# Prompt attention of a two-layer decoder step: one f32 triangle product per step replaced by two fp32r products of a split operand

## The reference, cut to what matters

```python
def stick_breaking_block(q, k, v, bias, q_pos, k_pos):
    z = (jnp.einsum('bqhd,bkhd->bhqk', q, k).astype(jnp.float32) * (SB_HEAD_DIM ** -0.5)
         + bias.astype(jnp.float32)[None, :, None, None])
    mask = k_pos[None, :] < q_pos[:, None]
    log_keep = jnp.where(mask, jax.nn.log_sigmoid(-z), 0.0)
    between = lax.cumsum(log_keep, axis=3, reverse=True) - log_keep
    a = jnp.where(mask, jnp.exp(jax.nn.log_sigmoid(z) + between), 0.0)
    return jnp.einsum('bhqk,bkhd->bqhd', a.astype(v.dtype), v)
```

## Time and profile before

| | |
|---|---|
| median of 3 runs | 2942.45 us (2940.32 to 2943.23) |
| profiled execution | 2944.57 us |
| its span, first to last instruction | 2942.9 us |
| TensorE busy | 2762.6 us, 94% |
| VectorE busy | 1578.4 us, 54% |
| ACT busy | 968.1 us, 33% |
| POOL busy | 678.6 us, 23% |

### The profile page before, as it was taken

One profiled execution on the slowest core, in us unless ns is written; L12 is line 12 of the kernel. 1 busy time (PEld: TensorE's weight loads), 2 busy tenths in 40 slices (PEclk: granted clock), 3 DMA queues, 4 the chain that ended last, 5 costly groups with the idle time before them and its releaser, 6 DMA issues. The chain is left out here.

```text
span 2942.9 us, 45906 instructions
## 1 busy us (share of the span) xinstructions
PE 2762.6 (94%) x17051; PEld 2367.5 (80%) x17051; DVE 1578.4 (54%) x2496; ACT 968.1 (33%) x1747; POOL 678.6 (23%) x624
## 2 busy tenths in 40 slices
PE   7999999988898899999989999999989999999898
PEld 7988888734444699799749999999967769999567
DVE  5367777788656677452334434333448963351534
ACT  5311121245565111332233323333334442231231
POOL 0001222222231222220002225422237612220020
PEclk9999999989999999999999999999999999999999
DMA  7477998787614711321654233323268864314641
GB/s 271 141 250 250 348 347 315 255 258 224 179 40 150 252 51 30 114 84 52 230 194 136 83 107 120 108 95 107 96 206 274 275 220 166 103 63 154 209 157 66
DMA packets 300161, 498.86 MB, mean 170 GB/s; under 512 B 45113, under 2 KB 175802, under 8 KB 299586
## 3 DMA queue, kind: packets, MB, share of 16 engines
q1 hardware_dynamic: 280642, 429.13, 44.1%
q0 software_dynamic: 15120, 51.46, 5.1%
q10 hardware_dynamic: 4176, 15.32, 1.3%
HBM read 383.06 MB, written 117.00 MB: 170 GB/s over the span
## 5 line engine op out<-in xcount | busy, mean ns | idle before, releaser
L889 PE MATMUL ps<-in_hi,w_halves 128*128 128x344 f32 x1536 | 499.6, 325 | 13.3 <-DVE in_lo L800 13.3
L891 PE MATMUL ps<-in_hi,w_halves 128*128 128x344 f32 x1536 | 494.5, 322 | 0.0
L890 PE MATMUL ps<-in_lo,w_halves 128*128 128x344 f32 x1536 | 494.1, 322 | 0.0
L647 POOL TENSOR_TENSOR w_halves<-w_raw,w_halves 128x1024 fp32r<-128x1024 f32 x60 | 145.9, 2435 | 727.3 <-ACT w_halves L720 727.3
L889 PEld LDWEIGHTS ps<-in_hi,w_halves 128*128 128x128 f32 x1536 | 292.5, 190 | 20.7 <-DVE in_lo L800 19.6
L890 PEld LDWEIGHTS ps<-in_lo,w_halves 128*128 128x128 f32 x1536 | 292.0, 190 | 1.1
L891 PEld LDWEIGHTS ps<-in_hi,w_halves 128*128 128x128 f32 x1536 | 292.2, 190 | 0.0
L1937 PE MATMUL ps<-in_hi,wv_hi 128*128 128x344 f32 x696 | 229.3, 329 | 3.9 <-DVE wv_lo L1785 3.9
L1938 PE MATMUL ps<-in_lo,wv_hi 128*128 128x344 f32 x696 | 224.3, 322 | 0.0
L1939 PE MATMUL ps<-in_hi,wv_lo 128*128 128x344 f32 x696 | 224.2, 322 | 0.0
L488 PE MATMUL ps<-in_hi,w_halves 128*128 128x344 f32 x640 | 204.7, 320 | 0.4 <-DVE w_halves L364 0.4
(11 more groups left out here) (428 smaller groups left out, 6100.9 us busy)
## 6 DMA issues: line engine op xcount, KB each, us to landing
k_pages<-in_cache_k SPq DMA_DIRECT2D x256, 256.0 KB, 4.7
v_pages<-in_cache_v POOLq DMA_DIRECT2D x160, 256.0 KB, 5.5
v_pages<-in_cache_v SPq DMA_DIRECT2D x96, 256.0 KB, 3.0
w_raw<-in_w_c SPq DMA_DIRECT2D x48, 512.0 KB, 3.8
in_raw<-og SPq DMA_DIRECT2D x120, 172.0 KB, 3.5
cc<-residual SPq DMA_DIRECT2D x120, 172.0 KB, 1.9
kq_raw<-in_w_mem SPq DMA_DIRECT2D x32, 512.0 KB, 4.0
w_words<-in_mem_k SPq DMA_DIRECT2D x16, 1024.0 KB, 5.9
```

The source lines that it names most:

```text
L647: return eng.tensor_tensor(w_lo[:, m % KT, :], raw[:, m % RAW, :], w_hi[:, m % KT, :].bitcast(f32), ALU.subtract)
L889: pe.matmul(acc(n), w_hi[:, t, a:b], h, start=(kt == 0), stop=False)
L890: pe.matmul(acc(n), w_hi[:, t, a:b], l, start=False, stop=False)
L891: last = pe.matmul(acc(n), w_lo[:, t, a:b], h, start=False, stop=(kt == KT - 1))
```

## The change

The softplus of a step is split in two. ACT copies it into `sp_hi`, which rounds it to fp32r; the pool engine subtracts that from the softplus into `sp_lo`. The triangle's f32 product becomes two fp32r products, of `sp_hi` and of `sp_lo`, with an fp32r copy of the triangle. The sum waits for `sp_lo`. VectorE's softplus waits for the subtraction of step t-3 in place of the sum. In its round t, ACT does the copy of step t+1 between weight(t-1) and logarithm(t+3). The pool engine does the subtraction of a step ahead of that step's additions.

```diff
-                pe.wait_ge(sp_done, t + 1)
-                last = pe.matmul(o, k.c("neg_tri"), sp_[:, t % 3, n0:512], start=False, stop=top(t), skip_group_check=True)
+                pe.wait_ge(sp_lo_done, t + 1)
+                pe.matmul(o, tri_r[:, :], sp_hi[:, t % 3, n0:512], start=False, stop=False, skip_group_check=True)
+                last = pe.matmul(o, tri_r[:, :], sp_lo[:, t % 3, n0:512], start=False, stop=top(t), skip_group_check=True)
...
-            pe.wait_ge(tables_done, 2)
+            pe.wait_ge(tables_done, 3)
...
-                    dve.wait_ge(sum_done, t - 2)
+                    dve.wait_ge(sp_lo_done, t - 2)
...
+            def softplus_high(t):
+                n0 = n0_of(t)
+                act.wait_ge(sp_done, t + 1)
+                if t >= 3:
+                    act.wait_ge(sum_done, t - 2)
+                act.copy(sp_hi[:, t % 3, n0:512], sp_[:, t % 3, n0:512]).then_inc(sp_hi_done, 1)
...
-            for dst, src in ((ident_r, k.c("ident")), (mask_r, k.sb_mask[:, :])):
+            for dst, src in ((ident_r, k.c("ident")), (mask_r, k.sb_mask[:, :]), (tri_r, k.c("neg_tri"))):
                 act.copy(dst[:, :], src).then_inc(tables_done, 1)
...
             for t in range(3):
                 logarithm(t)
+                if t == 1:
+                    softplus_high(0)
...
                     if t >= 1:
                         weight(t - 1)
+                    if t + 1 < NT_:
+                        softplus_high(t + 1)
                     if t + 3 < NT_:
                         logarithm(t + 3)
...
+            def softplus_low(t):
+                n0 = n0_of(t)
+                pool.wait_ge(sp_hi_done, t + 1)
+                if t >= 3:
+                    pool.wait_ge(sum_done, t - 2)
+                pool.tensor_tensor(sp_lo[:, t % 3, n0:512], sp_[:, t % 3, n0:512], sp_hi[:, t % 3, n0:512].bitcast(f32),
+                                   ALU.subtract).then_inc(sp_lo_done, 1)
+
             for t in range(NT_):
+                softplus_low(t)
                 if not last_block(t):
                     later(t)
```

More of the change, by code:

```diff
@@ L1005, in sb_prompt @@
         vtok = sb("vtok", [128, 2, T // 128, 128])
-        ident_r, mask_r = (sb(n, [128, 128], f32r) for n in ("ident_r", "mask_r"))
+        ident_r, mask_r, tri_r = (sb(n, [128, 128], f32r) for n in ("ident_r", "mask_r", "neg_tri_r"))
         zc = sb("zc", [128, 3, 512])
         sp_ = sb("softplus", [128, 3, 512])
+        sp_hi, sp_lo = sb("softplus_hi", [128, 3, 512], f32r), sb("softplus_lo", [128, 3, 512], f32r)
         acc = sb("later_blocks", [128, 4, 512])
@@ L1013, in sb_prompt @@
         v_in, gate_in, tables_done, vt_done, vtok_done = (sem(x) for x in ("v_in", "gate_in", "tables", "vt_done", "vtok"))
-        z_done, zc_done, e_done, l_done, sp_done = (sem(x) for x in ("z", "zc", "e", "l", "sp"))
+        z_done, zc_done, e_done, l_done, sp_done, sp_hi_done, sp_lo_done = (
+            sem(x) for x in ("z", "zc", "e", "l", "sp", "sp_hi", "sp_lo"))
         acc_done, sum_done, a_done, av_done, og_done, stored, zeroed = (
```

## The result

The changed kernel takes 2948.47 us (median of 11 runs, 2946.12 to 2953.58) where the kernel before, timed beside it, takes 2942.01 (11 runs): a ratio of 1.0020, with a 95% interval of 1.0012 to 1.0028. It is slower by 6.5 us, little but clear of no change, where 3.1 us of gain was forecast; the time itself lies within the stated range of 2930.5 to 2950. The profiled execution has a span of 2946.5 us against 2942.9.

The account below looks back on a forecast made before the run. Transfers set some 156 of the stage's 312 us, computing the rest, with TensorE the bound from 784 to 889. Terms 0, -0.2, 0, -0.4, -1.5, -1.0 made -3.1: 2939.4 us against 2942.45, range 2930.5 to 2950.

Parts of the forecast that it names:

- Rival 4: Triangle products not one-pass, or reloading weights at 0.37 us: nothing saved, +4 us, 2946.4; within the forecast's 0.54.
- Page stretches: 577 to 658 and 685 to 749 us, set by page transfers: 0 change (0 to +2, 0 to +1).
- Rival 3: Held products of pages overrun the spare 3.25 and 4.40 us: +3 us, 2945.4; within the forecast's 0.54.
- the walk: Fourteen steps from 835 us followed through four queues: first full-width sum 0.6 us later; page products go before subtractions.
- 784 to 835: Stretch with page values: -1.5 us (-4.6 to +3.5); full steps gain up to 0.37, narrow steps lose.
- the narrow steps of 835 to 889: Last pair's steps of 128 to 384 columns: a small loss, +0.6 us.
- The loop: Sum, exponent, cast, subtraction with four hand-overs at 0.1: 4.3 us in two steps, 2.15 a step, under 2.55.
- Full-width steps: Last pair's 512-column steps, 835 to 889 us: -2.9 us with perfect hand-over, of which -1.6 was left.
- the floor of 2.55 a step: Pool engine's two operations in a full-width step take 2.55 us, against TensorE's 2.78 before and 2.41 after.
- the sign of 2.5 to 2.65: Full steps of the last pair at 2.5 to 2.65 us would show the forecast right.
- rival 1: TensorE's saving reaches the end: 4.6 + 6.3 us from 784, 1 per short stretch, -12.9, 2929.6; chance 0.25.
- Rival 2: The sum's chain is the new bound, TensorE waiting from 784 us: forty-one steps by 0.2, +8.2, 2950.7; chance 0.21.

Follow-up runs that it names:

- e1_beside: Changed kernel, but cast and subtraction go unused: the f32 triangle product stays and waits for the softplus alone; ratio 0.9995 to the kernel before.
- e10_not_last: The change in pairs 0 to 2 alone; the last pair keeps the one f32 product of the kernel before; ratio 1.0007 to the kernel before.
- e11_last_alone: The change in the last pair alone, its order unaltered; pairs 0 to 2 as in the kernel before; ratio 1.0006 to the kernel before.
- e5: Changed kernel with the carried product first, then the rounded part's, then the remainder's, each behind its own wait; ratio 0.9994 to the kernel before.
- e7: Changed kernel with, in the last pair alone, ACT's cast moved up between exponential and logarithm of the round before; ratio 1.0010 to the kernel before.
- e8: Changed kernel, pairs 0 and 1 as before the change; in pairs 2 and 3 VectorE makes the rounded part, carried product first; ratio 0.9993 to before.
- e9: Changed kernel with the carried product first in all pairs and, in the last pair, the cast between exponential and logarithm; ratio 0.9993 to the kernel before.
- e12: Kernel before, with the change in the last pair alone, carried product first and cast between exponential and logarithm; ratio 0.9994 to the kernel before.
- e3_free_split: Changed kernel without cast, subtraction or remainder: VectorE writes the softplus rounded, the second one-pass product is of zeros; ratio 0.9979 to the kernel before.

## Why the prediction went wrong, point by point

- One-pass products: right. At 512 columns they start 0.23 us apart, and over the stage TensorE's busy time fell by 15.8 us of the 25.3, at a lower granted clock (0.90 for 0.94 on the mean), which lengthens products. Rival 4 is out:

```profile
743.52 0.40 PE L1106 MATMUL ps<-softplus_hi,neg_tri_r 128*128 128x512 f32 x1
743.75 0.39 PE L1107 MATMUL ps<-softplus_lo,neg_tri_r 128*128 128x512 f32 x1
743.98 1.02 PE L1111 MATMUL ps<-later_blocks,consts_sb 128*128 128x512 f32 x2
```

- Page stretches, forecast 0 (0 to +2, 0 to +1): the last value pages reach TensorE 1.1 and 1.6 us later, counted from the first page transfer, still on the DMA wait, 2.92 and 3.15 us. Within the doubt named above. Rival 3 is out.
- Prices: casts 611, 504, 398 and 289 ns for 616, 505, 394 and 283. The pool engine's busy time rose by 115.8 us over the stage (85.8 to 201.5) for 96; the subtractions meet VectorE's two-input products, which the forecast took at nothing, and take 1438 ns on the mean at 512 columns for 1275 (1280 from 784 on, where there are no such products):

```profile
L1421 POOL TENSOR_TENSOR softplus_lo<-softplus,softplus_hi 128x512 fp32r<-128x512 f32 x48 | 69.0, 1438 | 46.2 <-ACT softplus_hi L1348 39.8 <-PE ps L1111 6.0
```

  As the walk had it, the products of pages go first; their mean even fell, from 2642 to 2410 ns. The one that is held is the subtraction: ten of the 96 ran beside a product and took 1.9 us more on the mean than others of their width. By e1_beside that costs nothing that shows.
- 784 to 835, forecast -1.5, and the narrow steps of 835 to 889, forecast +0.6: these are the steps that failed. By the marks, step 72 stands 1.4 us later against the first cast (not shown to be the wait's own, as said of e10_not_last; but nothing is gained there), and steps 72 to 86 take 4.1 us more, 2.4 of them at full clock in e11_last_alone. The loop priced the cast as if it began 0.1 us after its softplus or its exponent; it began 1.33 later on the mean, and the walk with four hand-overs missed it: in these blocks ACT runs without a gap (843.39 to 849.6 in the trace), because the exponentials and logarithms of the next, wider steps stand among the narrow ones. That ACT had time left over the whole stretch (36.89 of 54 us) said nothing of this.
- Full-width steps, forecast -1.6: 0.0 (20.7 to 20.7 us for eight). Here the pool engine is the pace, as the floor of 2.55 a step had it. In the kernel after it idles 0.5 of the 20.65 us between the subtractions of steps 86 and 94, and nothing in e5, e7, e8, e9 and e12, where the same eight steps take it 20.1:

```profile
874.38 1.29 POOL L1421 TENSOR_TENSOR softplus_lo<-softplus,softplus_hi 128x512 fp32r<-128x512 f32 x1
875.62 1.31 POOL L1413 TENSOR_TENSOR later_blocks<-later_blocks,softplus 128x512 f32<-128x512 f32 x1
876.86 1.30 POOL L1421 TENSOR_TENSOR softplus_lo<-softplus,softplus_hi 128x512 fp32r<-128x512 f32 x1
```

  What failed is what the floor was compared with: 2.78 is the pace of steps with a full carried product and next scores. Of the eight steps the first two carry 384 columns and the last two have no next scores, and their mean was 2.59 already. So the sign of 2.5 to 2.65 was met by luck, with nothing gained. The cast waited here too, 1.57 us on the mean of steps 86 to 95 (0.09 in e7_cast_between), which the 0.5 us of idle time bound. Without subtractions, in e3_free_split, the eight steps take 17.6, which the pool engine's 20.1 doesn't allow the orders that subtract there.
- The saving's ceiling, 10.9 us from 784 on in rival 1: e3_free_split gives 5.7 in the last pair and 4.5 at the end.
- Rival 2, the slower one, had the mechanism, and came near in size: TensorE before the sum from 784 on, +8.2 us, 2950.7; measured 2948.47. Its trigger was put wrongly, on hand-overs of 0.3 or a late pool engine; it is ACT's order. Its sign, over 20 us of wait, came out at 16.8 on the weight loads and 9.3 on the products: the bar was too high. That the size fits is luck, since the full-width steps lose nothing and the loss is not spread over forty-one.
- The last sign, a granted clock that drops from 784 on, was there too: 0.97 for 1.00 in both rows. Its share is told in the last section.
- Behind the stage both kernels are the same; of the stage's +7.2 the span shows +3.6, for the stage began 1.4 us earlier, and what follows it was 2.2 shorter in that execution.

## What to carry to other kernels

A step that goes from one hand-over to three is priced by the place of each new instruction in its engine's program, not by its duration: look at what stands ahead of it when its input is ready, in the stretch where that engine runs without a gap. Compare the new chain with the time at which the waiting engine takes the result up now (here 2.55 us after the softplus); here a chain below that was free. If such a split is wanted, put the casting instruction where its input comes, and let the waiting engine do its independent work first: either move returned here, in the trace, what the change had lost in the last pair. Then look for the next floor: here it was the pool engine's two operations, 2.48 us of a full-width step, and no order of the rest went below it.

## What was not expected of the hardware

The granted clock, 1.00 from 784 to 889 before, fell to half in two stretches of 3.4 us after. Windows around the second, columns as in the first table:

```profile
846.00:850.20 4.20, 3.03 (x18) 2.03 (x17) 2.03 (x5) 4.13 (x10) 3.77 (x5) 1.00 0.11 17
850.20:853.60 3.40, 3.40 (x8) 1.04 (x7) 0.00 (x0) 1.47 (x4) 1.59 (x2) 0.50 0.00 0
```

TensorE had been 3.03 of 4.20 us busy before it, with the wait of 1.17 us shown above as its last gap, and was then granted 0.50, its 1.2 GHz level. That the wait brought the fall is not shown, for e11_last_alone has waits of the same kind, of up to 1.2 us, and this clock:

```profile
835.00:889.00 54.00, 47.63 (x188) 25.21 (x188) 26.37 (x44) 43.79 (x87) 41.78 (x51) 1.00 0.07 21
```

The half clock is not the whole loss (K): e11_last_alone loses 2.4 us in the narrow steps at 1.00, and e3_free_split is the fastest with 6.8 us of half clock at 785. But it is a part. TensorE was busy for all of the 3.40 us, and a triangle product took 0.43 us from start to next start (850.38 to 850.81) for 0.23 at full clock. So about half of it, 1.7 us, is added, an estimate from these rows, and that is what lies between the 4.1 us lost in the narrow steps of the kernel after and the 2.4 of e11_last_alone. No run changed the clock by itself. In the timed runs the clock over the whole span was 0.974 on the mean for the kernel after and 0.977 to 0.978 for the one before; it was 0.974 for e3_free_split too, so what it costs the whole program stays open.
